# Layer 0 of a two-layer mixture-of-experts backbone: tokens sorted once per tile, pieces copied together by VectorE

## The reference

```
sel = sigmoid(t @ router_w) + router_b           # 16 experts in 4 groups
# best group, then the best two experts in it; gates = their scores over their sum
for e in range(16):
    he = silu(t @ w_gate[e]) * (t @ w_up[e])     # 1024 -> 512
    y = y + gates[:, e:e + 1] * (he @ w_down[e]) # 512 -> 1024
```

## Time and profile before

| | us |
|---|---|
| median of 3 runs | 1154.78 (1153.63 to 1155.25) |
| the profiled execution | 1155.82 |
| its span, from the first to the last instruction | 1154.1 |
| TensorE busy in the span | 997.5 |
| VectorE busy | 463.6 |
| ScalarE busy | 336.5 |
| GpSimd busy | 35.0 |

### The profile page before, as it was taken

One profiled execution on the slowest core, in us unless ns is written; L12 is line 12 of the kernel. 1 busy time (PEld: TensorE's weight loads), 2 busy tenths in 40 slices (PEclk: granted clock), 3 DMA queues, 4 the chain that ended last, 5 costly groups with the idle time before them and its releaser, 6 DMA issues.

```text
span 1154.1 us, 26812 instructions
## 1 busy us (share of the span) xinstructions
PE 997.5 (86%) x10945; PEld 627.6 (54%) x10946; DVE 463.6 (40%) x1250; ACT 336.5 (29%) x788; POOL 35.0 (3%) x65
## 2 busy tenths in 40 slices
PE   5699989898987899999999984799988885866997
PEld 3244645433436467676666654486667653443554
DVE  1455666665125322222222224486852542232343
ACT  3322155554014122222222222424751311111121
POOL 0000000000000000000000002000000000000000
PEclk9899999998995899999999995899999798897999
DMA  8992099798211079796888877204213299999961
GB/s 327 427 376 101 3 378 375 266 388 346 85 61 85 6 275 411 279 414 243 346 341 342 352 309 275 93 1 153 86 50 152 92 411 428 428 428 429 429 283 36
DMA packets 28720, 297.53 MB, mean 258 GB/s; under 512 B 4944, under 2 KB 6240, under 8 KB 11776
## 3 DMA queue, kind: packets, MB, share of 16 engines
q1 hardware_dynamic: 22976, 285.49, 60.8%
q0 software_dynamic: 3984, 11.15, 3.0%
q10 hardware_dynamic: 1712, 0.23, 0.1%
HBM read 288.85 MB, written 15.86 MB: 264 GB/s over the span
## 4 chain that ended last, share of the span: by engine, by line
PE 74%; DMA 11%; DVE 8%; ACT 3%; issue 3%; ACTq 1%; POOL 0%; SPq 0%; DVEq 0%; POOLq 0%
PE bank L647 18%; PE bank L464 10%; DMA ring<-in_w_up_dram 9%; PE bank L659 8%; PE bank L635 8%; PE bank L564 7%; PE bank L534 4%; PE bank L407 3%; PE bank L505 3%; PE bank L517 2%; PE bank L598 2%; DVE h_t L1104 1%; PE bank L688 1%; PE bank L473 1%; PE bank L452 1%
## 5 line engine op out<-in xcount | busy, mean ns | idle before, releaser
L647 PE MATMUL bank<-ring,h_t 128*32 128x256 f32 x4160 | 253.4, 398 | 54.7 <-DMA ring<-in_w_up_dram 35.2
L647 PEld LDWEIGHTS bank<-ring,h_t 128*32 128x32 f32 x4160 | 159.2, 115 | 142.6 <-issue 81.3
L464 PE MATMUL bank<-h_t,ring 128*128 128x512 f32 (+1 forms) x320 | 118.1, 524 | 12.5 <-ACT h_t L813 12.5
L659 PE MATMUL bank<-ring,h_t 128*32 128x256 f32 x2080 | 125.8, 380 | 2.1 <-ACT h_t L912 2.1
L1284 DVE TENSOR_TENSOR h_t<-h_t,bank 128x128 f32<-128x128 f32 x65 | 18.7, 288 | 264.5 <-ACT h_t L905 264.5
L635 PE MATMUL bank<-tokm,h_t 128*32 128x256 f32 x1760 | 110.7, 385 | 8.5 <-DVE h_t L1258 8.5
L912 ACT COPY h_t<-bank 32x256 f32 x168 | 61.3, 365 | 150.4 <-PE bank L659 81.1
L905 ACT ACTIVATE h_t<-bank 128x128 f32<-128x128 f32 x65 | 18.1, 278 | 283.8 <-PE bank L647 283.8
L659 PEld LDWEIGHTS bank<-ring,h_t 128*32 128x32 f32 x2080 | 73.6, 110 | 42.2 <-issue 10.2
L464 PEld LDWEIGHTS bank<-h_t,ring 128*128 128x128 f32 x320 | 62.5, 196 | 60.9 <-issue 40.6
L635 PEld LDWEIGHTS bank<-tokm,h_t 128*32 128x32 f32 x1760 | 67.1, 111 | 37.4 <-issue 9.9
(11 more groups left out here) (168 smaller groups left out, 1008.8 us busy)
## 6 DMA issues: line engine op xcount, KB each, us to landing
ring<-in_w_gate_dram SPq DMA_DIRECT2D x32, 2048.0 KB, 10.5
ring<-in_w_up_dram SPq DMA_DIRECT2D x32, 2048.0 KB, 14.1
ring<-in_w_down_dram SPq DMA_DIRECT2D x32, 2048.0 KB, 14.3
ring<-in_ada_w_dram SPq DMA_DIRECT2D x24, 2048.0 KB, 10.1
ring<-in_w_in_dram SPq DMA_DIRECT2D x8, 1536.0 KB, 21.0
y_rows<-in_table_dram SPq DMA_DIRECT2D x1, 8704.0 KB, 57.6
ring<-in_w_out_dram SPq DMA_DIRECT2D x4, 2048.0 KB, 9.3
y_rows<-h_t POOLq DMA_DIRECT2D x42, 128.0 KB, 6.1
```

The costliest lines, as they stand in the source:

```text
L464: last = mm(bank[1 + i % 2][:, 0:widths[i]], qk_weights(i, k), h_t[:, k, 0:widths[i]], start=(k == 0), stop=(k == KD - 1))
L647: last = mm(o.rearrange("r (s c i) -> r s c i", s=2, c=KF), hc_t[:, k, :], w[:, :, k, :, CHUNK * q:CHUNK * q + CHUNK], start=(k == 0), sto ...
L659: last = mm(bank[4][CHUNK * q:CHUNK * q + CHUNK, 0:256], he_t[:, k, :], wd[:, k, 256 * q:256 * q + 256], start=(k == 0), stop=(k == KF - 1))
```

## The change

TensorE sorts each of the four token tiles by expert once: a product of the tile's columns with a 0/1 matrix 128x256 (each token at the place of its first and of its second expert). ScalarE copies the results to `rows_buf`, where a sorted tile is 8 blocks of 256 columns. Bases and counts give, per piece and tile, one column at which the piece's tokens start in that tile, packed with the column of the window at which they go (64 x source + column); `where` holds 4 numbers per piece. In the loop `fill_window` copies 32 columns from each tile into `window`, each copy over the end of the one before, so that the next tile's tokens cover what was too much. `rows_in` copies the window to `hc_t`. `pick_rows`, `pick` and `rows_turned` stay for layer 1 only. `window`, `iota`, `hc_t` and others lie over constants of the attention, which SyncE loads again behind layer 0. `row_out` is now one copy of 128x256 into one buffer, stored by a DMA that ScalarE itself issues; GpSimd's loop of stores goes.

```diff
+        rows_buf = sb("rows_buf", [P, 8 * D + C_END])
+        h_t = rows_buf[:, 0:4 * D].rearrange("p (k n) -> p k n", k=KD)
+        tokm = rows_buf[:, 4 * D:8 * D].rearrange("p (t n) -> p t n", t=4)
+        cst = rows_buf[:, 8 * D:8 * D + C_END]
...
+                    sp.wait_ge(fills_done, 1)
+                    sp.dma_start(spare, table[:, C_BLK:C_G]).then_inc(cst_in, 16)
                     sp.wait_ge(yg_in[3], 32)
...
+                for tt in range(nt):
+                    pe.wait_ge(hot_ready, tt + 1)
+                    if tt == nt - 1:
+                        pe.wait_ge(table_ready, 1)
+                        for t2 in range(nt):
+                            last = mm(bank[6][0:1, P * t2:P * t2 + P], table_cols[:, t2:t2 + 1], ident,
+                                      start=True, stop=True)
+                        last.then_inc(table_mm, 1)
+                    for half in range(2):
+                        i = 2 * tt + half
+                        if i >= 3:
+                            pe.wait_ge(sort_out, i - 2)
+                        for k in range(4 * half, 4 * half + 4):
+                            last = mm(bank[2 * (i % 3) + k % 4 // 2][:, 256 * (k % 2):256 * (k % 2) + 256],
+                                      tokm[:, tt, P * k:P * k + P], tile_hot[tt % 2], start=True, stop=True)
+                        last.then_inc(sort_mm, 1)
...
                     gate_up(g0, a)
-                    pick_rows(g0 + 1)
                     if prev is not None:
                         down(g0 - 1, prev)
                     with pe.Fori(g0 + 1, g1) as g:
                         gate_up(g, a)
-                        pick_rows(g + 1)
                         weights_in(a, turns, (2,))
                         down(g - 1, a)
...
                 def row_out(g):
                     act.wait_ge(down_mm[l], g + 2)
-                    act.wait_ge(rows_stored[0], (g + 2) // 2 * 16)
-                    act.wait_ge(rows_stored[1], (g + 3) // 2 * 16)
-                    for q in range(4):
-                        last = nc.scalar.copy(yrow[:, bass.ds(g % 2 * D + 256 * q, 256)],
-                                              bank[4][CHUNK * q:CHUNK * q + CHUNK, 0:256])
-                    last.then_inc(rows_ready, 1)
+                    act.wait_ge(rows_stored, (g + 1) * 16)
+                    nc.scalar.copy(y_out0, bank[4][:, 0:256]).then_inc(rows_ready, 1)
+                    act.wait_ge(rows_ready, g + 2)
+                    act.dma_start(y_rows[bass.ds(CHUNK * g, CHUNK), :].rearrange("r (q c) -> q r c", q=4),
+                                  y_out0).then_inc(rows_stored, 16)
...
+            def sorted_rows(first_pieces, positions):
...
+                hot(0)
+                hot(1)
+                dve.wait_ge(base_mm, 1)
+                first_pieces(bank[7][:, 3 * NE:4 * NE])
+                hot(2)
...
+                hot(3)
+                positions(bank[7][:, 128:192])
+                weights(0)
+                dve.wait_ge(table_mm, 1)
+                v.tensor_copy(where.rearrange("p (t g) -> p t g", t=4),
+                              bank[6][0:1, :].rearrange("p (t g) -> p t g", t=4)[:, :, 0:GT]).then_inc(where_ready, 1)
+
+            def fill_window(n):
+
+                for t in range(4):
+                    packed = dve.value_load(where[0:1, bass.ds(n + GT * t, 1)], min_val=0, max_val=64 * 256 + CHUNK)
+                    rows = rows_buf[:, bass.ds(packed // 64 + 2 * D * t, 2 * D)].rearrange("p (k n) -> p k n", k=KD)
+                    col = nc.s_assert_within(packed % 64, 0, CHUNK,
+                                             skip_runtime_bounds_check_because="table_cols adds at most CHUNK to a multiple of 64")
+                    copied = v.tensor_copy(window[:, :, bass.ds(col, CHUNK)], rows[:, :, 0:CHUNK])
+                    if t < 3:
+                        copied.then_inc(fill_step, 1)
+                        dve.wait_ge(fill_step, 3 * n + t + 1)
+                copied.then_inc(window_ready, 1)
+
+            def sorted_experts():
+
+                def rows_in(n):
+                    dve.wait_ge(window_ready, n + 1)
+                    v.tensor_copy(hc_t[0], window[:, :, 0:CHUNK]).then_inc(hc_ready[0], 1)
+
+                dve.wait_ge(where_ready, 1)
+                dve.wait_ge(sort_out, 2 * TOK_TILES[0])
+                fill_window(0)
+                rows_in(0)
+                dve.wait_ge(hc_ready[0], 1)
+                fill_window(1)
+                total = all_chunks(dve, 0)
+                with dve.Fori(0, total) as g:
+                    dve.wait_ge(silu_done[0], g + 1)
+                    v.tensor_tensor(he[0], act_g[0], bank[1][:, P:2 * P], ALU.mult).then_inc(he_ready[0], 1)
+                    dve.wait_ge(gu_mm[0], g + 1)
+                    rows_in(g + 1)
+                    dve.wait_ge(he_ready[0], g + 2)
+                    dve.wait_ge(down_mm[0], g + 1)
+                    v.transpose(he_flat[0], he[0]).then_inc(het_ready[0], 1)
+                    dve.wait_ge(het_ready[0], g + 1)
+                    dve.wait_ge(hc_ready[0], g + 2)
+                    fill_window(g + 2)
+                dve.wait_ge(window_ready, total + 2)
+                dve.sem_inc(fills_done, 1)
```

More of the change, by code:

```diff
@@ L199, in backbone @@
         hits = hflat[:, 128:384].rearrange("p (m r) -> p m r", r=CHUNK)
[L200 to L203, removed]
-        pos = work[:, 736:744]
-        yrow = hflat[0:CHUNK, 2048:4096]
+        spare = cst[:, C_BLK:C_G]
+        iota = spare[:, 0:256]
+        tile_hot = [spare[:, 256:512], spare[:, 512:768]]
+        window = spare[:, 256:768].rearrange("p (k r) -> p k r", k=KD)
+        hc_flat = [spare[:, 768:1024], hflat[:, 768:1024]]
+        hc_t = [a.rearrange("p (k r) -> p k r", k=KD) for a in hc_flat]
+        act_g = [work[:, 1280:1408], hflat[:, 1024:1152]]
+        he = [spare[:, 0:128], hflat[:, 1152:1280]]
+        he_flat = [spare[:, 128:256], hflat[:, 1280:1408]]
+        he_t = [a.rearrange("p (k r) -> p k r", k=KF) for a in he_flat]
+        pos = work[:, 736:744]
+        y_out0 = work[:, 1024:1280]
+        less_b = work[:, 0:64].bitcast(BF16).rearrange("p (s t e) -> p s t e", s=2, t=4)
+        table_cols = work[:, 836:840]
+        where = work[0:1, 0:4 * GT].bitcast(I32)
+        tile_rows = [rows_buf[:, 2 * D * t:2 * D * t + 2 * D].rearrange("p (k n) -> p k n", k=KD) for t in range(4)]
         ych = [tokm, hflat.rearrange("p (t n) -> p t n", t=4)]
@@ L360, in _ @@
                 sp.wait_ge(pv_done, sum(UNITS[:l + 1]) // 4)
+                if l == 0:
+                    sp.dma_start(iota, table[:, C_IOTA:C_ALL]).then_inc(iota_in, 16)
                 load_expert(l, 2, 2, (1, 2))
@@ L764, in _ @@
                         ada_turn(u)
+                else:
+                    pe.wait_ge(cst_in, 32)
                 qkv(l)
@@ L993, in _ @@
         def _(pool):
-            pool.wait_ge(block_zeroed, 1)
-            for turns in (1, 2):
-                for i in range(turns - 1, 2):
-                    pool.dma_start(y_rows[ROWS:ROWS + CHUNK, :].rearrange("r (q c) -> q r c", q=4),
-                                   ring[:, 8, 0:256]).then_inc(rows_stored[i], 16)
-                    pool.wait_ge(rows_stored[i], 16 * turns)
+            pool.sem_inc(rows_stored, 16)
             for l in range(DEPTH):
@@ L1386, in _ @@
                 route(l)
-                experts(l)
                 if l == 0:
+                    sorted_experts()
                     combine(l)
+                else:
+                    experts(l)
             dve.wait_ge(scattered, all_chunks(dve, DEPTH - 1) + 1)
```

271 lines of the change are left out of this document (171 added, 100 removed).

## The result

The changed kernel takes **1242.7 us** (median of 4 runs, 1241.8 to 1244.6) against 1155.0 for the kernel before on the same chip: ratio 1.0759, 95% interval 1.0737 to 1.0781. The profiled execution has a span of 1240.6 us, 86.5 more than before. The kernel is slower, as forecast, but 1242.7 lies 62 us above the end of the range.

A forecast was written before the change was run, and what follows sets the result against it. TensorE bounds the kernel before; VectorE's queue was to bound the changed loop at 7.0 us a piece. The gather comes 3.9 us later: 1155.8 + 3.9 = 1159.7, the median 1.0 lower, so 1159 us; range 1138 to 1181.

The forecast's parts named there:

- Stores of rows: Expert loop, one buffer stored by ScalarE: round 7.05 us beside weights, 3.1 without, mean under the period, no cost.
- Rival C: Expert loop: the store's round bounds, 8.3 us at its worst, 7.5 mixed, time 1179; chance 0.12.
- VectorE replaces TensorE as the bound: Expert loop: VectorE's queue sets the period at 7.0 us, instead of TensorE's 6.91 plus gaps; chance 0.52.
- The step: One of four window copies in `fill_window`: read, check, addresses, copy and semaphore, 1.47 us (1.28 to 1.73).
- rival A: `fill_window`: cheaper steps of 1.345 us through short address operations, period 6.5, time 1139, faster; chance 0.29.
- First gate product 397.6: Before the loop: sorting, first window fill and copy to `hc_t` start the first gate product 15.1 us later than 382.51.
- Weights no bound in the loop: Expert loop, a sign of the forecast: no wait for weights in the loop.
- Rival D, the clock: Expert loop: TensorE's clock falls as it idles 1.8 us per piece; 1295 if it lasts at 0.50; chance 0.03.
- Wrong if TensorE waits for ScalarE's copy of the rows: Expert loop: one of three signs named in advance that would show the forecast wrong; no size given.
- Rival B: Expert loop: reads and checks hide behind copies, TensorE bounds at 5.6 us a piece, time 1104; chance 0.04.
- the band: Whole kernel: 0.2%, 2.3 us, counted as no change; 0.11 us of period around 6.90; chance 0.12.
- faster 0.34: Whole kernel: the chance given to the changed kernel being faster, against 0.54 for slower.

The follow-up runs named there:

- no_stores: Changed kernel with the 42 row stores of layer 0 left out; 1120.4 us, ratio 0.9724 to the kernel before.
- pool_1k_2: Changed kernel with stores issued by GpSimd, one transfer per piece, from two buffers in turn; 1135.9 us, ratio 0.9846 to the kernel before.
- pool_2k_2: Changed kernel with stores issued by GpSimd, two transfers of 32 rows of 2 KB per piece, two buffers in turn; 1133.9 us, ratio 0.9810.
- pool_1k: Changed kernel with GpSimd instead of ScalarE issuing the same store from the same single buffer; 1211.5 us, ratio 1.0504 to the kernel before.
- act_1k_16: Changed kernel with each store issued by ScalarE as four transfers of 32 packets of 1 KB over 16 engines; 1193.1 us, ratio 1.0305.
- hoist_chk: pool_2k_2 with the next window start read and its addresses worked out before the wait for the current copy; 1113.1 us, ratio 0.9627.
- hoist: hoist_chk without the bounds check behind each of the four reads; 1103.3 us, ratio 0.9568 to the kernel before.

## Why the prediction was wrong

The failed step is **"Stores of rows"**: "one round: 0.38 + 0.2 + 6.1 + 0.35 = 7.05 us beside weights", and from it "no cost in the forecast". The 6.1 of the earlier trace rows is the landing of 32 packets of 4 KB spread over 16 engines. The change kept the bytes and altered the rest: 128 packets of 1 KB, on 4 engines. Beside weights that landing was mostly 15.7 to 24.3; the first such round took 16.9 (16.31 and 0.57 to the next issue), more than twice the piece of 6.24. I carried a duration over by bytes. Rival C had the right mechanism, but priced it with the same row, at its worst 7.4, and so reached only 1179.

That the kernel came out slower, as forecast, was luck: the cause forecast for it, VectorE's period, makes the kernel faster when no store holds it (no_stores, 0.9724).

Against the forecast, from the profiled execution (gather 699.7 forecast, 782.42 measured, +82.7):

| term | forecast | measured | difference |
|---|---|---|---|
| first copy to `hc_t` | 397.3 | 393.3 | -4.0 |
| 42 intervals without the stores' wait | 7.9 + 41 x 7.0 = 294.9 | 262.9 (no_stores) | -32.0 |
| the stores' wait in these 42 | 0 | 376.2 - 262.9 | +113.3 |
| last copy to gather | 7.5 | 12.9 (7.0 in no_stores) | +5.4 |

The points in turn:
- *VectorE replaces TensorE as the bound*: right where stores don't hold (no_stores, `<- issue` 166 times).
- *The step*, 1.47 us forecast: 1.36. The read's 0.76 was 0.07 + 0.31 + 0.19 + 0.02 and hand-overs, 0.72; addresses 0.2 to 0.25 instead of 0.30; the copy 0.295 instead of 0.354, faster than either row that I had bounded it by. With the ends of a piece at 0.8 instead of 1.12 the period was 6.24 to 6.26. Within the bounds of the step, and in size rival A, even below its 6.5. With the stores out of the way the kernel is 1.5 to 2.8% faster than before (pool_1k_2, no_stores), not 0.4% slower.
- *First gate product 397.6*: 393.61, of which 4.2 us come from the sorting that began at 371.07 instead of 375.3. A tile took 3.5 to 3.7, not 3.45; the order of the steps held.
- *Weights no bound in the loop*: right; no wait for `ring` in the changed kernel's loop.
- *Rival D, the clock*: it did fall, to 0.83 to 0.87, but behind stalls of up to 14 us for the stores. The idle time that D named (1.8 us a piece forecast, about 1 us measured) left it at 1.00.
- *Wrong if TensorE waits for ScalarE's copy of the rows*: this is what came, 104.6 us of it.
- *Rival B*, "against it: the wait on `fill_step` stands ahead of the next read": true of the kernel as written. With the read ahead of the wait B's state came, at 5.56 us a piece for its 5.6. That 1103.3 meets its 1104 to the microsecond is luck in part: the first copy came at 394.8 instead of 397.3 and the 42 intervals took 233.6 instead of 237.5, but the gather followed the last copy by 15.2 instead of 8.9.
- *Small slips in the sums*, none of which moves the result: the round adds up to 7.03, not 7.05; 699.7 - 695.87 is 3.8, not 3.9; and A and B together are 0.33, from which the band still takes a part, so "faster 0.34" is too much.

How the 122 us of the stores divide, by steps between runs: one transfer on 4 engines instead of four on 16 costs 50 (1242.7 to 1193.1); one buffer instead of two costs 76 (1211.5 to 1135.9, both by GpSimd, on 4 engines); that the stores are there at all, 10 to 16 (pool_2k_2 and pool_1k_2 against no_stores, by ratios and by times). They are steps along different paths and needn't add up. pool_1k is 18 us slower than act_1k_16 although their long landings are alike; its shortest is 3.8 us against 1.5.

Open: what fills the 4 us between a store's issue and its first packet when weights stream (1.2 us when they don't), and why the loop begins at 393 in some of these kernels and at 399 in others. How the landing grows with the packets of an engine is told only roughly: by the longest landings a further large packet costs some 0.5 us, an estimate from (10.9 - 8.0) / 6 and (24.3 - 10.9) / 24, near the 0.58 us between two packets in the store of 444.88. A store during which the weights pause is shorter.

## What to carry to other kernels

The landing of a transfer can't be taken from another with the same bytes: count its packets, and how many engines carry them, before a row is used for it. The DMA share in a stretch where nothing else moves tells the second (0.25 and 0.89 here). A single buffer costs its whole round as soon as the round is longer than a piece; a second one takes a slow landing off the path without making it any faster, as long as the piece is longer than half a round and than the time that the store's own packets take. And where an engine's queue reads a register between two dependent copies, put the read ahead of the wait.

## What the hardware showed that I had not expected

- An idle time of the kind that recurs in each piece (about 1 us in 6.26) left the granted clock at 1.00; stalls of up to 13.7 us brought the stretches to 0.83 to 0.87.
- A store's packets took turns with the weights' about one for one: 32 on an engine needed 18.1 us in a full stream, with packets of the weights of 0.61 us in between. 8 on an engine landed in at most 10.9 to 11.7 us, 2 in at most 8.0.
- Two stores of GpSimd under way together landed in 10.4 us each (median), but their packets followed each other; only the 4 us ahead of the packets overlapped.
- The same access pattern, 128 rows of 1 KB onto 32 of 4 KB, became 128 packets of 1 KB when ScalarE issued it, and 32 of 4 KB with 96 of 16 B when GpSimd did, on 4 engines both times (DMA share 0.25 and 0.23).
- The copy of 128x256 from SBUF to SBUF takes 0.295 us, the TENSOR_SCALAR of the same size 0.354.
- A bounds check behind a register read costs 0.19 us of VectorE's queue and an assert 0.02; four of each a piece were worth 9.8 us of the kernel (hoist_chk to hoist).
